# The up-projections of a latent attention as rounded high and low parts, with their weights earlier in the ring

## The chip, the cores and the metric

The kernel runs on one core of a Trainium2 chip, as one program. The time is that of one execution on the device, in microseconds (us); less is better. A core has TensorE (PE: matmuls, with the loads of their weights as PEld), VectorE (DVE), ScalarE (ACT), GpSimd (POOL) and SyncE (SP, which here issues the transfers from memory). Each engine runs its own instructions in order; between engines they wait for each other through counting semaphores.

## The reference

The program runs 512 tokens of width 1024, in float32, through two blocks. The first has two layers, each a projection of the normed input into 19 parts, four mixers beside each other (latent attention, differential attention, sparse attention with an index, a short convolution), gates, and an output projection. The second block (gated feed-forward, attention, attention to a memory, gated feed-forward) is not touched here. What is touched is the start of the latent attention:

```python
def _mla(cq, ckv, krope, qa_g, w_uq, kva_g, w_ukv, cos, sin):
    B, S, _ = cq.shape
    H = GROUP_HEADS                                     # 4
    q = (_rmsnorm(cq, qa_g) @ w_uq).reshape(B, S, H, MLA_NOPE + MLA_ROPE)       # 256 -> 4 x (64 + 32)
    ...
    kv = (_rmsnorm(ckv, kva_g) @ w_ukv).reshape(B, S, H, MLA_NOPE + MLA_V)      # 128 -> 4 x (64 + 64)
    k_nope, v = kv[..., :MLA_NOPE], kv[..., MLA_NOPE:]
```

The latents `cq` (256 wide) and `ckv` (128 wide) are parts of the first projection. The three products with `w_uq` and the two halves of `w_ukv` are the up-projections.

## The kernel before

**Matmuls.** Nearly all projections are made from rounded parts: a float32 operand is split into a high part, rounded to the format that TensorE multiplies in one go (`rounded(...)`, fp32r in the profile), and a low part, the rounded rest; three matmuls (high by high, high by low, low by high) add up to the product. The up-projections are the exception: they multiply plain float32 (`up_q`, `up_k`, `up_v`).

**The ring of weights.** Weights come in blocks of 128 x 1024 into a ring of four slots (`ring`). `TAKE` is the order of a layer's 44 blocks, so the slot of a block is its place in `TAKE` modulo four, and SyncE fetches block i + 4 when the job that used block i is done (`SLOT_JOB`). ScalarE makes the high part of a block (`whi`, two buffers, L1876), GpSimd its low part in two halves of 512 columns (L839), written over the block in its slot (`wlo` lies on `ring`). The blocks of the up-projections (`UK`, `UV`, `UQ`) are in `RAW`: no parts are made of them.

**Jobs.** A layer starts with fixed jobs (QI0, QI1 for the index, KR, CQ0, CQ1, CKV for the latents, BQ0, BK0, VT0). Then come 34 steps (`s`), each with the attention of some units (scores, transposes of the probabilities, products with the values) and fills: pieces of further projections from the list `FILLERS`, dealt out by a planner (`fill_plan`). Both kernels have the same plan. Step 0 is filled with BQ1; step 1 with UK0, UK1, UV0, UV1 and the start of BK1; step 2 ends BK1, copies a block of values (VN0) and starts VT1; then come UQ0 and UQ1, GT0 (gate block 0), UQ2.

**What sets the order around the change.** The scores of step s wait until the row minima of step s - 1 are taken (`min_ready`), which VectorE does. VectorE's first minimum in layer 0 waits until GpSimd has set the mask of the bias tables, which it does behind BK1's low part:

```python
dve.wait_ge(bias1_masked, 2)                       # ahead of step 0's minima
...
prepare_after("VT0")                               # on POOL: BK1's low part
if L == 0:
    mask_bias1()
after_low(SLOT_OF["BK1"])
```

The scores of step 2 use banks in which UK1 and UV0 lay, and wait for ScalarE's copies of these (`up_out`). VectorE scales the latents by their norms (L2601, `latent_ready`) before the up-projections.

Of the kernel before, what the change touches and what calls it, by code (L numbers as in the profile page):

```python
# [75 lines left out]
TAKE = ("QI0", "QI1", "KR", "KI", "CQ0", "CQ1", "CKV", "BQ0", "BK0", "VT0", "BQ1", "BK1", "UK", "UV", "VT1", "UQ",  # L76
# [14 lines left out]
SLOT_JOB = [JOB[{"UQ": "UQ2", "UK": "BK1", "UV": "BK1", "KI": "KR"}.get(name, name)] for name in TAKE]  # L91
# [220 lines left out]
LAYER_KA, LAYER_QA, LAYER_UP = 12, 7, 5  # L312
# [105 lines left out]
def build(nc, x, wstream, params, gains, tab1, tab2, hot1, hot2, rope, ident_in, mem, lines1, lines2, out):  # L418
    ctx = ExitStack()
    with ctx:  # L420
# [83 lines left out]
        cqn, ckvn = cqT, ckT[:, 0, :]  # L504
        at_v = at[0]
        vA, vBC = view(NT, 4 * HD), view(NT, 8 * HD)
        dBC = view(4, S)
# [312 lines left out]
        def _(pool):  # L820
# [69 lines left out]
            def layer(L):  # L890
# [36 lines left out]
                pool.wait_ge(kA_ready, L * LAYER_KA + 4)  # L927
# [27 lines left out]
                def low_a(which, h):  # L955

                    if which == "K" and h < 2:
                        pool.wait_ge(up_out, L * LAYER_UP + 5)
# [100 lines left out]
        def _(pe):  # L1059
# [113 lines left out]
            for L in range(DEPTH):  # L1173
# [39 lines left out]
                def turn_v(n):  # L1213

                    wait_out(pe, L, f"VT{n}")
                    if n == 0:
                        pe.wait_ge(up_out, L * LAYER_UP + 4)
# [76 lines left out]
                def up_q(n):  # L1294

                    w, b = raw_slot("UQ"), proj[bank_of(L, f"UQ{n}")]
                    pe.wait_ge(uq_loaded, 80 * (L + 1))
                    bank_free(f"UQ{n}")
                    for k in range(2):
                        block = 2 * ((n + 2) % 3) + k  # L1300
                        mm = pe.matmul(b[:, :], w[:, block * P:(block + 1) * P], cqn[:, k, :], start=(k == 0), stop=(k == 1))  # L1301
                    mm.then_inc(job_done, 1)

                def up_k(pair):

                    w, b = raw_slot("UK"), UP_BANK[f"UK{pair}"]
                    pe.wait_ge(latent_ready, L * 3 + 3)
                    pe.matmul(b[:, :], w[:, pair * P:(pair + 1) * P], ckvn, start=True, stop=True).then_inc(up_done, 1)

                def up_v(half):  # L1310

                    w, b = raw_slot("UV"), UP_BANK[f"UV{half}"]
# [44 lines left out]
                def scores(s):  # L1357
# [10 lines left out]
                    if s == B_STEPS:  # L1368
                        wait_out(pe, L, "UQ1", "UQ2")
                        pe.wait_ge(kA_ready, L * LAYER_KA + 8)  # L1370
                    if s == B_STEPS + 4:
                        pe.wait_ge(kA_ready, L * LAYER_KA + 12)
# [4 lines left out]
                    if quad_step(s):  # L1377
                        if s == 2:
                            pe.wait_ge(up_out, L * LAYER_UP + 3)
# [472 lines left out]
        def _(act):  # L1852
# [81 lines left out]
            for L in range(DEPTH):  # L1934
# [89 lines left out]

                prepare_after("VT0")
# [17 lines left out]
                def high_a(which, pair):  # L2043

                    heads = slice(2 * pair, 2 * pair + 2)
                    if which == "K":
                        act.wait_ge(up_out, L * LAYER_UP + (pair + 1))
                        act.wait_ge(kA_ready, L * LAYER_KA + 4)
# [62 lines left out]
                for s in range(LAST_STEP):  # L2111
# [268 lines left out]
        def _(dve):  # L2380
# [111 lines left out]
            for L in range(DEPTH):  # L2492
# [112 lines left out]
                stage_v(0)  # L2605

# [45 lines left out]
                def o_out(o):  # L2652
# [3 lines left out]
                    if branch == "B":  # L2656
                        if pair == 0:
                            dve.wait_ge(kA_ready, L * LAYER_KA + 4)
# [557 lines left out]
```

## Time and profile before

| | us |
|---|---|
| median of 3 runs | 1757.62 |
| lowest, highest | 1757.21, 1757.74 |
| profiled execution, its own time | 1759.74 |
| its span, from the first to the last instruction | 1757.9 |
| TensorE busy | 1749.2 |
| VectorE busy | 1032.4 |
| ScalarE busy | 757.8 |
| GpSimd busy | 421.5 |

Busy times are those of the profiled execution. Its mean granted TensorE clock is 0.998 of full speed. TensorE holds 99% of the chain of work that ended last. A matmul's row shows its whole passage, and successive ones overlap; the distance of two starts says what one costs in a steady flow.

### The profile page before, as it was taken

Reading aid. Unit: us, or ns where it says so; the run is one execution under the profiler, and the core shown is the slowest. Engines: PE = TensorE matmul, PEld = TensorE weight load, DVE = VectorE, ACT = ScalarE, POOL = GpSimd, SP = SyncE. Lnnn points to the kernel's source line nnn. Section 1 sums busy time; section 2 is a strip of 40 time slices with the busy share of each in tenths; the row PEclk is TensorE's granted clock in tenths of the full one; section 3 lists DMA queues with packets and bytes.
Section 4 is the critical chain, followed back from the end, with each engine's and each line's share of the span. In section 5 each row is a group of like instructions: output and inputs, shape, how many; then the busy total and the mean of one; then the engine's idle time right before and its main releaser. Section 6 shows DMA issues by size and latency. Waiting matters only on the chain.

```text
span 1757.9 us, 25383 instructions
## 1 busy us (share of the span) xinstructions
PE 1749.2 (100%) x9298; PEld 1435.9 (82%) x9298; DVE 1032.4 (59%) x2170; ACT 757.8 (43%) x1396; POOL 421.5 (24%) x326
## 2 busy tenths in 40 slices
PE   9999999999999999999999999999999999999998
PEld 7778878777887888888888888889888888888887
DVE  4888776688877665555433455445756655555333
ACT  6466644546564523233233455556434322222222
POOL 4545553454644500000000332330200200000000
PEclk9999999999999999999999999999999999999999
DMA  6432123323212343333333422223322333333332
GB/s 192 129 100 73 49 65 93 96 68 105 73 49 73 103 132 96 98 96 98 102 108 103 155 61 84 85 84 109 96 73 61 91 100 97 95 95 95 102 103 94
DMA packets 54421, 166.18 MB, mean 95 GB/s; under 512 B 10200, under 2 KB 10712, under 8 KB 54328
## 3 DMA queue, kind: packets, MB, share of 16 engines
q1 hardware_dynamic: 53032, 162.12, 30.6%
q10 hardware_dynamic: 1296, 2.84, 0.5%
q8 instruction: 56, 0.92, 0.2%
q14 instruction: 37, 0.30, 0.1%
HBM read 162.25 MB, written 2.17 MB: 94 GB/s over the span
## 4 chain that ended last, share of the span: by engine, by line
PE 99%; DMA 0%; DVE 0%; ACT 0%; ACTq 0%; POOL 0%; issue 0%; DVEq 0%
PE proj L1113 80%; PE turned L1427 2%; PE o L1449 2%; PE proj L1591 1%; PE proj L1584 1%; PE o L1692 1%; PE o L1792 1%; PE score L1397 1%; PE turned L1079 1%; PE turned L1671 1%; PE score L1781 1%; PE proj L1301 1%; PE turned L1654 1%; PE score L1386 1%; PE score L1654 0%; PE score L1269 0%
## 5 line engine op out<-in xcount | busy, mean ns | idle before, releaser
L1113 PE MATMUL proj<-hhi,whi 128*128 128x512 f32 x1456 | 582.6, 400 | 0.0
L1113 PE MATMUL proj<-hhi,wlo 128*128 128x512 f32 x1456 | 568.4, 390 | 0.0
L1113 PE MATMUL proj<-hlo,whi 128*128 128x512 f32 x1456 | 567.4, 390 | 0.0
L1876 ACT ACTIVATE whi<-ring 128x1024 fp32r<-128x1024 f32 x279 | 295.4, 1059 | 623.7 <-PE proj L1113 602.3
L2384 DVE TENSOR_TENSOR wlo<-ring,whi 128x1024 fp32r<-128x1024 f32 x199 | 243.2, 1222 | 161.2 <-ACT whi L1876 160.7
L1113 PEld LDWEIGHTS proj<-hhi,whi 128*128 128x128 f32 x1456 | 274.0, 188 | 63.6 <-issue 10.4
L1113 PEld LDWEIGHTS proj<-hhi,wlo 128*128 128x128 f32 x1456 | 273.4, 188 | 58.6
L1113 PEld LDWEIGHTS proj<-hlo,whi 128*128 128x128 f32 x1456 | 274.1, 188 | 53.5 <-issue 0.7
L839 POOL TENSOR_TENSOR wlo<-ring,whi 128x512 fp32r<-128x512 f32 x160 | 215.5, 1369 | 339.9 <-ACT whi L1876 339.9
L857 POOL TENSOR_TENSOR prob<-prob 128x512 f32<-128x512 f32 x36 | 56.9, 1581 | 872.2 <-ACT prob L1872 872.2
L1902 ACT ACTIVATE prob<-prob,negmax 128x256 f32<-128x256 f32 (+3 forms) x208 | 114.0, 550 | 74.1 <-DVE negmax L2457 73.4
L1113 PE MATMUL proj<-inner_hi,whi 128*128 128x512 f32 x352 | 136.9, 389 | 0.0
L1113 PE MATMUL proj<-inner_lo,whi 128*128 128x512 f32 x352 | 136.9, 389 | 0.0
L1113 PE MATMUL proj<-inner_hi,wlo 128*128 128x512 f32 x352 | 136.9, 389 | 0.0
L2457 DVE CUSTOM_DVE_ANT_0 prob<-score,arena 128x256 f32<-128x256 f32 (+3 forms) x148 | 60.6, 446 | 72.9 <-PE score L1654 61.0
L2468 DVE TENSOR_TENSOR tmp<-proj,R 128x512 f32<-128x512 f32 x48 | 33.2, 691 | 117.4 <-PE proj L1113 115.1
L1113 PE MATMUL proj<-yhi,whi 128*128 128x512 f32 x245 | 96.7, 395 | 0.1
L1113 PE MATMUL proj<-yhi,wlo 128*128 128x512 f32 x245 | 95.7, 390 | 0.0
L1113 PE MATMUL proj<-ylo,whi 128*128 128x512 f32 x245 | 95.2, 389 | 0.0
L2813 DVE TENSOR_TENSOR tmp<-tmp,proj 128x512 f32<-128x512 f32 x44 | 30.3, 688 | 103.7 <-PE proj L1113 103.5
L1113 PEld LDWEIGHTS proj<-inner_hi,wlo 128*128 128x128 f32 x352 | 66.1, 188 | 13.8
L1113 PEld LDWEIGHTS proj<-inner_hi,whi 128*128 128x128 f32 x352 | 66.1, 188 | 13.8
(379 smaller groups left out, 2436.9 us busy)
## 6 DMA issues: line engine op xcount, KB each, us to landing
ring<-wstream SPq DMA_DIRECT2D x285, 512.0 KB, 3.6
arena<-lines SPq DMA_DIRECT2D x28, 256.0 KB, 5.7
arena<-x ACTq DMA_DIRECT2D x4, 512.0 KB, 6.3
out<-arena SPq DMA_DIRECT2D x8, 256.0 KB, 2.9
arena<-mem SPq DMA_DIRECT2D x1, 1024.0 KB, 8.5
ring<-wstream SPq DMA_DIRECT2D x12, 64.0 KB, 2.2
ring<-wstream ACTq DMA_DIRECT2D x2, 256.0 KB, 7.7
arena<-rope SPq DMA_DIRECT2D x4, 128.0 KB, 6.4
```

The source lines that it names most:

```text
L839: return pool.tensor_tensor(rounded(wlo[:, s, cols]), ring[:, s, cols], whi[:, h, cols], ALU.subtract)
L857: pool.tensor_tensor(sq[:, 3, :], sq[:, 0, :] if c == 1 else sq[:, 3, :], sq_last if c == KC - 1 else sq[:, c % 3, :], ALU.add).then_inc(s ...
L1079: mm = pe.matmul(to[:, col + n * t:col + n * (t + 1)], chunk[:, t * P:(t + 1) * P], w, start=(first and t == 0), stop=False, skip_group_ch ...
L1113: mm = pe.matmul(b, rounded(w), rounded(rhs(v, k)), start=(first and n == 0 and p == 0), stop=(last and n == len(blocks) - 1 and p == 2))
L1427: mm = pe.transpose(turn_bank(g)[:, kb * P:(kb + 1) * P], prob[:, (2 * s + n) % 4, kb * P:(kb + 1) * P], ident[:, :])
L1449: mm = pe.matmul(opsum[o % 2][h * HD:(h + 1) * HD, qb * P:(qb + 1) * P], v, pT[:, (g - 1 + h) % 4, kb * P:(kb + 1) * P], start=(kb == 0), ...
L1876: act.activation(rounded(dst), src, ACT.Copy, scale=scale).then_inc(ready, 1)
L1902: act.activation(prob[:, i, 0:W], prob[:, i, 0:W], ACT.Exp, bias=negmax[:, i:i + 1], scale=-1.0, accum_out=rowsum[:, i:i + 1] if total is ...
L2384: dve.tensor_tensor(rounded(wlo[:, s, :]), ring[:, s, :], whi[:, h, :], ALU.subtract).then_inc(lo_ready, 1)
L2457: dve.tensor_tensor_reduce(prob[:, i, 0:W], src[:, 0:W], bias, 1.0, 3e38, ALU.add, ALU.min, negmax[:, i:i + 1]).then_inc(min_ready, 1)
L2468: return dve.tensor_tensor(dst, src, factors, ALU.mult)
L2813: dve.tensor_tensor(tmp[:, s, :], tmp[:, s, :], proj[(j + 1) % 2][:, :], ALU.mult)\
```

## The change

The three up-projections are made from rounded parts like the others: each plain matmul becomes three rounded ones (`up_q`: 2 to 6 in a job; `up_k`: 1 to 3; `up_v`: 2 to 6). For this ScalarE rounds the latents and the three weights, VectorE makes the low parts of the key latent and of the keys' and values' weights, GpSimd those of the query latents and the queries' weights. The high parts lie where factors of the norm lay, the low parts of the weights in their ring slots. In `TAKE`, UK and UV move ahead of BK1, so BK1's block goes from slot 3 to slot 1 and is fetched when VT0 is done, no longer when BQ0 is; the slots of UK and UV are free for UQ and GT0 once UK and UV are done. The semaphores' counts grow accordingly.

```diff
-TAKE = ("QI0", "QI1", "KR", "KI", "CQ0", "CQ1", "CKV", "BQ0", "BK0", "VT0", "BQ1", "BK1", "UK", "UV", "VT1", "UQ",
+TAKE = ("QI0", "QI1", "KR", "KI", "CQ0", "CQ1", "CKV", "BQ0", "BK0", "VT0", "BQ1", "UK", "UV", "BK1", "VT1", "UQ",
...
-SLOT_JOB = [JOB[{"UQ": "UQ2", "UK": "BK1", "UV": "BK1", "KI": "KR"}.get(name, name)] for name in TAKE]
+SLOT_JOB = [JOB[{"UQ": "UQ2", "UK": "BQ1", "UV": "BQ1", "KI": "KR"}.get(name, name)] for name in TAKE]
...
@@ gpsimd @@
                 after_low(SLOT_OF["BK1"])
                 pool.wait_ge(relu_ready, L * IDX_UNITS + IDX_UNITS)
+                pool.wait_ge(up_out, L * LAYER_UP + 4)
+                for k in range(2):
+                    pool.tensor_tensor(rounded(cqn_lo[:, k, :]), cqn[:, k, :], cqn_hi[:, k, :], ALU.subtract).then_inc(kA_ready, 1)
+                pool.wait_ge(kA_ready, L * LAYER_KA + 2)
                 for h in range(4):
                     pool.tensor_tensor(kA[rows, h, :], krope[rows, 0, :], krope[rows, 1, :], ALU.add).then_inc(kA_ready, 1)
...
+                def low_queries():
+
+                    slot = SLOT_OF["UQ"] % RING
+                    pool.wait_ge(up_out, L * LAYER_UP + 9)
+                    for cols in (slice(4 * P, 6 * P), slice(0, 4 * P)):
+                        pool.tensor_tensor(rounded(wlo[:, slot, cols]), ring[:, slot, cols], uq_hi[:, cols], ALU.subtract).then_inc(kA_ready, 1)
...
                         prepare_after(name)
+                        if name == "UV1":
+                            low_queries()
...
@@ tensor, up_q @@
-                    pe.wait_ge(uq_loaded, 80 * (L + 1))
+                    pe.wait_ge(kA_ready, L * LAYER_KA + (7 if n == 0 else 8))
...
-                        mm = pe.matmul(b[:, :], w[:, block * P:(block + 1) * P], cqn[:, k, :], start=(k == 0), stop=(k == 1))
+                        for p, (w, v) in enumerate(((uq_hi[:, cols], cqn_hi), (uq_hi[:, cols], cqn_lo), (wlo[:, slot, cols], cqn_hi))):
+                            mm = pe.matmul(b[:, :], rounded(w), rounded(v[:, k, :]), start=(k == 0 and p == 0), stop=(k == 1 and p == 2))
...
@@ tensor, up_k @@
-                    pe.wait_ge(latent_ready, L * 3 + 3)
-                    pe.matmul(b[:, :], w[:, pair * P:(pair + 1) * P], ckvn, start=True, stop=True).then_inc(up_done, 1)
+                    pe.wait_ge(latent_ready, L * LAYER_LATENT + 5)
+                    for p, (w, v) in enumerate(((uk_hi[:, cols], ckvn_hi), (uk_hi[:, cols], ckvn_lo), (wlo[:, slot, cols], ckvn_hi))):
+                        mm = pe.matmul(b[:, :], rounded(w), rounded(v), start=(p == 0), stop=(p == 2))
...
@@ tensor, up_v @@
+                    pe.wait_ge(latent_ready, L * LAYER_LATENT + 6)
                     for t in range(2):
-                        tok = (2 * half + t) * P
-                        mm = pe.matmul(b[:, t * 256:(t + 1) * 256], ckvn[:, tok:tok + P], w[:, 0:2 * P], start=True, stop=True)
+                        tok = slice((2 * half + t) * P, (2 * half + t + 1) * P)
+                        for p, (v, w) in enumerate(((ckvn_hi, uv_hi), (ckvn_hi, wlo[:, slot, 0:2 * P]), (ckvn_lo, uv_hi))):
+                            mm = pe.matmul(b[:, t * 256:(t + 1) * 256], rounded(v[:, tok]), rounded(w), start=(p == 0), stop=(p == 2))
...
@@ scalar @@
+                def high_queries():
+
+                    w = raw_loaded("UQ")
+                    act.wait_ge(uq_loaded, 80 * (L + 1))
+                    high(w[:, 0:6 * P], uq_hi, up_out)
+
+                act.wait_ge(latent_ready, L * LAYER_LATENT + 3)
+                high(ckvn, ckvn_hi, up_out)
+                high(raw_loaded("UK")[:, 0:2 * P], uk_hi, up_out)
+                high(raw_loaded("UV")[:, 0:2 * P], uv_hi, up_out)
+                high(cqn, cqn_hi, up_out)
                 prepare_after("VT0")
...
+                    if s == 1:
+                        high_queries()
...
@@ vector @@
                 stage_v(0)
+                dve.wait_ge(up_out, L * LAYER_UP + 1)
+                dve.tensor_tensor(rounded(ckvn_lo), ckvn, ckvn_hi, ALU.subtract).then_inc(latent_ready, 1)
+                for n, (name, w_hi) in enumerate((("UK", uk_hi), ("UV", uv_hi))):
+                    slot = SLOT_OF[name] % RING
+                    dve.wait_ge(up_out, L * LAYER_UP + (n + 2))
+                    dve.tensor_tensor(rounded(wlo[:, slot, 0:2 * P]), ring[:, slot, 0:2 * P], w_hi, ALU.subtract).then_inc(latent_ready, 1)
```

ScalarE's instructions between the jobs BK0 and BQ1 of layer 0, where the four new roundings come in. `wload0` to `wload3` say that the block in that ring slot has landed; the row with `whi` is BK1's rounding, the two rows after it are the exponentials of step 0. Before:

```order
L1876 ACTIVATE bk_hi_60<-arena 128x512 [waits job_free1]
L2017 ACTIVATE arena<-arena 128x2 [waits lam_step]
L1876 ACTIVATE whi<-ring 128x1024 [waits job_done,wload3]
L1902 ACTIVATE prob,arena<-prob,negmax 128x128 [waits min_ready]
L1902 ACTIVATE prob,rowsum<-prob,negmax 128x128 [waits min_ready]
```

and now:

```order
L1900 ACTIVATE bk_hi_60<-arena 128x512 [waits job_free1]
L2041 ACTIVATE arena<-arena 128x2 [waits lam_step]
L1900 ACTIVATE latent_hi_67<-arena 128x512 [waits latent_ready]
L1900 ACTIVATE factors2_53<-ring 128x256 [waits wload3]
L1900 ACTIVATE factors2_53<-ring 128x256 [waits wload0]
L1900 ACTIVATE latent_hi_67<-arena 128x1024
L1900 ACTIVATE whi<-ring 128x1024 [waits job_done,wload1]
L1926 ACTIVATE prob,arena<-prob,negmax 128x128 [waits min_ready]
L1926 ACTIVATE prob,rowsum<-prob,negmax 128x128 [waits min_ready]
```

BK1's rounding now stands behind four others and waits for another slot.

GpSimd's instructions of layer 0 from BK1's low part (the first two rows) to VT1's. The memsets set the mask, the rows of 32x512 are the rope sums. Before:

```order
L839 TENSOR_TENSOR wlo_49<-ring,whi 128x512 [waits hi_ready]
L839 TENSOR_TENSOR wlo_49<-ring,whi 128x512
L885 MEMSET arena 128x512
L888 MEMSET arena 64x13x64 [waits bias1_masked,bias1_loaded]
L926 TENSOR_TENSOR arena<-arena 32x512 [waits relu_ready,pool_lo_ready]
L926 TENSOR_TENSOR arena<-arena 32x512 x3
L945 TENSOR_TENSOR bq_lo_61<-arena,bq_hi_59 128x512 [waits bhi_ready,kA_ready]
L839 TENSOR_TENSOR wlo_49<-ring,whi 128x512 [waits hi_ready,b_ready]
L839 TENSOR_TENSOR wlo_49<-ring,whi 128x512
```

and now, up to the first low part of the queries' weights:

```order
L843 TENSOR_TENSOR wlo_49<-ring,whi 128x512 [waits hi_ready]
L843 TENSOR_TENSOR wlo_49<-ring,whi 128x512
L889 MEMSET arena 128x512
L892 MEMSET arena 64x13x64 [waits bias1_masked,bias1_loaded]
L931 TENSOR_TENSOR cq_lo_63<-arena,latent_hi_67 128x512 [waits up_out,relu_ready,pool_lo_ready]
L931 TENSOR_TENSOR cq_lo_63<-arena,latent_hi_67 128x512
L934 TENSOR_TENSOR arena<-arena 32x512 [waits kA_ready]
L934 TENSOR_TENSOR arena<-arena 32x512 x3
L960 TENSOR_TENSOR bq_lo_61<-arena,bq_hi_59 128x512 [waits bhi_ready,kA_ready]
L843 TENSOR_TENSOR wlo_49<-ring,whi 128x512 [waits hi_ready,b_ready]
L843 TENSOR_TENSOR wlo_49<-ring,whi 128x512
L942 TENSOR_TENSOR wlo_49<-ring,factors_52 128x256 [waits up_out]
```

Two subtractions come in between the mask and the rope sums, and two more behind VT1's low part.

## Rows read from the trace of the kernel before

**Rows 1.** The page's busy times: engine, us (share of the span), instructions.

```profile
PE 1749.2 (100%) x9298; PEld 1435.9 (82%) x9298; DVE 1032.4 (59%) x2170; ACT 757.8 (43%) x1396; POOL 421.5 (24%) x326
```

**Rows 2.** TensorE's waits after 60 us: line, releaser, total us, times, longest.

```profile
PE turned L1079 <- ACT pT L2206: 0.2, 1, 0.2
```

**Rows 3.** Chain of work, 50 to 130 us: start us, us, what.

```profile
75.42 5.67 PE proj L1113 x24
...
81.57 1.91 PE turned L1308 x4
83.48 1.73 PE o L1315 x8
85.21 3.41 PE proj L1113 x15
...
101.40 1.72 PE proj L1301 x4
```

**Rows 4.** Timeline of TensorE near 1070 us: start us, us, instruction.

```profile
1070.04 0.28 PE L1584 MATMUL proj<-memhi,wlo 128*128 128x256 f32 x1
1070.16 0.28 PE L1584 MATMUL proj<-memhi,whi 128*128 128x256 f32 x1
```

**Rows 5.** Timeline of TensorE, layer 0 and, last row, layer 1.

```profile
81.02 0.33 PE L1397 MATMUL score<-bk_hi,bq_hi 32*128 32x128 f32 x2
...
88.55 0.50 PE L1386 MATMUL score<-bk_hi,bq_hi 32*128 32x512 f32 x2
...
92.05 0.48 PE L1113 MATMUL proj<-hhi,whi 128*128 128x512 f32 x1
...
391.78 0.48 PE L1113 MATMUL proj<-hhi,whi 128*128 128x512 f32 x1
```

**Rows 6.** SyncE's issue, its time to landing, and all such loads.

```profile
74.97 0.33 SPq L751 DMA_DIRECT2D ring<-wstream  x1
...
ring<-wstream SPq DMA_DIRECT2D x1, 512.0 KB, 3.5
...
DMA to landing us min/median/max: 3.4/3.6/7.4
```

**Rows 7.** Timeline of ScalarE, layer 0; brackets: idle before, and its end.

```profile
75.03 1.06 ACT L1876 ACTIVATE whi<-ring 128x1024 fp32r<-128x1024 f32 x1 [4.16 <-PE proj L1113]
...
84.38 0.63 ACT L1876 ACTIVATE bq_hi<-arena 128x512 fp32r<-128x512 f32 x1 [3.03 <-DVE arena L2469]
...
87.34 0.60 ACT L2065 ACTIVATE arena<-o 128x512 f32<-128x512 f32 x1
```

**Rows 8.** Timeline of GpSimd, layer 0.

```profile
76.17 2.55 POOL L839 TENSOR_TENSOR wlo<-ring,whi 128x512 fp32r<-128x512 f32 x2 [3.75 <-ACT whi L1876]
...
79.31 0.79 POOL L888 MEMSET arena<- 64x832 f32 x1
80.17 4.97 POOL L926 TENSOR_TENSOR arena<-arena 32x512 f32<-32x512 f32 x4
85.22 1.29 POOL L945 TENSOR_TENSOR bq_lo<-arena,bq_hi 128x512 fp32r<-128x512 f32 x1
```

**Rows 9.** Timeline of VectorE, layer 0 and, last row, layer 1.

```profile
73.57 2.05 DVE L2601 SCALAR_TENSOR_TENSOR arena<-arena,par,turned 128x512 f32<-128x512 f32 x3
...
80.13 0.29 DVE L2457 CUSTOM_DVE_ANT_0 prob<-score,arena 128x128 f32<-128x128 f32 x1 [2.52 <-issue]
...
377.25 0.28 DVE L2457 CUSTOM_DVE_ANT_0 prob<-score,arena 128x128 f32<-128x128 f32 x1
```

**Rows 10.** TensorE's timeline; stretches: length, busy PE, PEld, DVE, ACT, POOL, granted clock.

```profile
194.79 1.84 PE L1079 MATMUL proj<-halves,tmp 128*128 128x2 f32 x16
...
190.00:200.00 10.00, 10.00 (x70) 8.73 (x69) 7.28 (x25) 4.22 (x10) 3.81 (x4) 0.90 0.20 56
200.00:210.00 10.00, 10.00 (x62) 8.28 (x61) 5.45 (x23) 7.62 (x24) 4.20 (x3) 0.93 0.10 19
490.00:500.00 10.00, 10.00 (x75) 8.67 (x74) 7.31 (x28) 4.42 (x10) 3.80 (x4) 1.00 0.19 54
```

More of the change, by code:

```diff
@@ L311 @@
          B_STEPS: (("K", 2), ("K", 3)), B_STEPS + 1: (("Q", 2),), B_STEPS + 2: (("Q", 3),)}
-LAYER_KA, LAYER_QA, LAYER_UP = 12, 7, 5
+LAYER_KA, LAYER_QA, LAYER_UP, LAYER_LATENT = 16, 7, 10, 6
 LAST_STEP = FILL_STEPS + 4
@@ L504, in build @@
         cqn, ckvn = cqT, ckT[:, 0, :]
+        cqn_lo, ckvn_lo = cq_lo, ck_lo[:, 0, :]
+        uk_hi, uv_hi, uq_hi = factors[1][:, 0, 0:2 * P], factors[1][:, 0, 2 * P:4 * P], factors[0][:, :, :].rearrange("p a b -> p (a b)")[:, 0:6 * P]
         at_v = at[0]
         vA, vBC = view(NT, 4 * HD), view(NT, 8 * HD)
+        latent_hi = over("latent_hi", "arena", [P, 3, S], at[0])
+        cqn_hi, ckvn_hi = latent_hi[:, 0:2, :], latent_hi[:, 2, :]
         dBC = view(4, S)
@@ L957, in low_a @@
                     if which == "K" and h < 2:
-                        pool.wait_ge(up_out, L * LAYER_UP + 5)
+                        pool.wait_ge(up_out, L * LAYER_UP + 10)
                     else:
@@ L1216, in turn_v @@
                     if n == 0:
-                        pe.wait_ge(up_out, L * LAYER_UP + 4)
+                        pe.wait_ge(up_out, L * LAYER_UP + 8)
                     if n == 1:
@@ L1300, in up_q @@
                         block = 2 * ((n + 2) % 3) + k
-                        mm = pe.matmul(b[:, :], w[:, block * P:(block + 1) * P], cqn[:, k, :], start=(k == 0), stop=(k == 1))
+                        cols = slice(block * P, (block + 1) * P)
+                        for p, (w, v) in enumerate(((uq_hi[:, cols], cqn_hi), (uq_hi[:, cols], cqn_lo), (wlo[:, slot, cols], cqn_hi))):
+                            mm = pe.matmul(b[:, :], rounded(w), rounded(v[:, k, :]), start=(k == 0 and p == 0), stop=(k == 1 and p == 2))
                     mm.then_inc(job_done, 1)
                 def up_k(pair):
-                    w, b = raw_slot("UK"), UP_BANK[f"UK{pair}"]
-                    pe.wait_ge(latent_ready, L * 3 + 3)
-                    pe.matmul(b[:, :], w[:, pair * P:(pair + 1) * P], ckvn, start=True, stop=True).then_inc(up_done, 1)
+                    slot, b = SLOT_OF["UK"] % RING, UP_BANK[f"UK{pair}"]
+                    cols = slice(pair * P, (pair + 1) * P)
+                    pe.wait_ge(latent_ready, L * LAYER_LATENT + 5)
+                    for p, (w, v) in enumerate(((uk_hi[:, cols], ckvn_hi), (uk_hi[:, cols], ckvn_lo), (wlo[:, slot, cols], ckvn_hi))):
+                        mm = pe.matmul(b[:, :], rounded(w), rounded(v), start=(p == 0), stop=(p == 2))
+                    mm.then_inc(up_done, 1)
                 def up_v(half):
-                    w, b = raw_slot("UV"), UP_BANK[f"UV{half}"]
+                    slot, b = SLOT_OF["UV"] % RING, UP_BANK[f"UV{half}"]
+                    pe.wait_ge(latent_ready, L * LAYER_LATENT + 6)
                     for t in range(2):
-                        tok = (2 * half + t) * P
-                        mm = pe.matmul(b[:, t * 256:(t + 1) * 256], ckvn[:, tok:tok + P], w[:, 0:2 * P], start=True, stop=True)
+                        tok = slice((2 * half + t) * P, (2 * half + t + 1) * P)
+                        for p, (v, w) in enumerate(((ckvn_hi, uv_hi), (ckvn_hi, wlo[:, slot, 0:2 * P]), (ckvn_lo, uv_hi))):
+                            mm = pe.matmul(b[:, t * 256:(t + 1) * 256], rounded(v[:, tok]), rounded(w), start=(p == 0), stop=(p == 2))
                     mm.then_inc(up_done, 1)
@@ L1369, in scores @@
                         wait_out(pe, L, "UQ1", "UQ2")
-                        pe.wait_ge(kA_ready, L * LAYER_KA + 8)
+                        pe.wait_ge(kA_ready, L * LAYER_KA + 12)
                     if s == B_STEPS + 4:
-                        pe.wait_ge(kA_ready, L * LAYER_KA + 12)
+                        pe.wait_ge(kA_ready, L * LAYER_KA + 16)
                     if s == C_STEP:
@@ L1378, in scores @@
                         if s == 2:
-                            pe.wait_ge(up_out, L * LAYER_UP + 3)
+                            pe.wait_ge(up_out, L * LAYER_UP + 7)
                         if quad_out(s) == 0 and quad_out(s - 2) == 1:
@@ L2023, in copy_v, with raw_loaded @@
                         .then_inc(v_copied, 1)
+                def raw_loaded(name):
+                    i = SLOT_OF[name]
+                    act.wait_ge(wload[i % RING], L * (16 * LAYER_SLOTS // RING) + 16 * (i // RING + 1))
+                    return ring[:, i % RING, :]
+                def high_queries():
[7 more added lines that the diff above has]
+                high(cqn, cqn_hi, up_out)
                 prepare_after("VT0")
@@ L2046, in high_a @@
                     if which == "K":
-                        act.wait_ge(up_out, L * LAYER_UP + (pair + 1))
-                        act.wait_ge(kA_ready, L * LAYER_KA + 4)
+                        act.wait_ge(up_out, L * LAYER_UP + (pair + 5))
+                        act.wait_ge(kA_ready, L * LAYER_KA + 6)
                         src, dst = kA[0:96, heads, :], kA_hi[pair][0:96, :, :]
```

6 lines of the change are left out of this document (3 added, 3 removed).

## The prediction

> **What bounds the kernel now.** Read the page first: TensorE is busy for 1749.2 of 1757.9 us [rows 1]. The list of waits then says whether it ever stands still: after the first 60 us it waited once, for 0.2 us [rows 2]. So the time is the sum of TensorE's instructions, in their order. What the change takes from them is gained, a wait that it adds there is paid in full, and work on the other engines counts only where TensorE comes to wait for it. The third view is the chain of work where the up-projections run in layer 0 [rows 3]; the fourth, the timelines of all engines from 70 to 103 us [rows 5 to 9], which tell how late each input may be. Layer 1 repeats them 299.7 us later (VT1 begins at 92.05 and at 391.78 [rows 5]), without the two memsets of the bias mask, which only layer 0 has.
>
> **TensorE's own work.** Today the two keys' jobs take 1.91 us and the two values' jobs 1.73 us [rows 3]. Of the 3.64, 0.21 is the passage out of the scores before them: behind the same kind of scores 24 rounded matmuls took 5.67 us, while 15 in steady flow took 3.41, or 0.227 each, and 5.67 - 24 x 0.227 = 0.21. That passage stays; 3.43 us goes. In its place come six rounded matmuls of 512 columns, 6 x 0.227 = 1.36, and twelve of 256 columns, whose starts lie 0.12 us apart elsewhere [rows 4], 1.44. Gain 0.63 us. A job of the queries takes 1.72 us [rows 3] and becomes six matmuls of 512: 1.36, a gain of 0.36, three times in a layer: 1.08. Both layers: 2 x (0.63 + 1.08) = **3.4 us less TensorE work**. Were nothing late, the change would gain that, 0.19%.
>
> **What comes late: BK1's weights.** In the ring's old order BK1's block was fetched when BQ0 was done, three jobs before its rounding; now it is fetched when VT0 is done. That issue, UV's today, stands at 74.97 us, and landed 3.5 us later [rows 6], at 78.5. ScalarE's rounding of BK1, which today begins at 75.03 [rows 7], so begins at 78.5: 3.5 us late. ScalarE's four new roundings stand ahead of it, but they are done by then: the scaled latents are ready at 73.57 + 2.05 = 75.6 [rows 9]; a rounding of 512 columns takes 0.63 us and one of 1024 columns 1.06 [rows 7], so with 0.63 as the bound for each of the two narrow ones all four end by 75.6 + 3 x 0.63 + 1.06 = 78.6 at most. They cost nothing as long as the load is the later one.
>
> GpSimd works in order, and behind BK1's rounding stands its low part (76.17 us today) and then, in layer 0, the memsets of the bias mask, which end at 80.10 [rows 8]. VectorE's first row minimum waits for just that by the program (the profile names no releaser): it starts at 80.13 after 2.52 us of idling [rows 9]. All this moves by 3.5 us, to 83.6, and the two minima of step 0, 0.28 us each, end at about 84.1. TensorE's scores of step 1 wait for these minima by the program; today they start at 81.02 [rows 5] with the minima done by 80.7. They will start at about 84.2: **layer 0 loses 3.2 us**, with TensorE idle. Layer 1 has no mask; there the three new subtractions of VectorE move its first minimum from 377.25 [rows 9] by some 1.5 us to 378.8, and its scores of step 1, at 81.02 + 299.7 = 380.7, still have over a microsecond to spare.
>
> **The second wait of layer 0.** The scores of step 2 need the copies of both keys' jobs and of one values' job out of PSUM; the last ends at 87.34 + 0.60 = 87.94 [rows 7] and the scores start at 88.55 [rows 5]. These copies stand behind a rounding that waits for VectorE [rows 7], and VectorE's line is now 3.5 us late, so they end at 91.44. TensorE comes there at 88.55 + 3.2 - 0.63 = 91.1: a wait of 0.4 us, which takes most of the 0.63 back.
>
> **The wait of layer 1: VT1's low part.** On GpSimd two subtractions of the queries' latents come in, ahead of the four rope sums and of VT1's low part. In the clock times of layer 0, mask left out: BK1's rounding ends at 78.5 + 1.06 = 79.6, its low part takes 2.55 us (to 82.2), the new pair 2 x 1.29 (as BQ1's low part [rows 8], the same shape; to 84.8), the rope sums 4.97 (to 89.8), BQ1's low part 1.29 (to 91.1), the first half of VT1's low part half of 2.55 (to 92.4). TensorE wants VT1 at 92.05 - 0.63 = 91.4 [rows 5]. **Layer 1 waits about 1.0 us**, 1.1 with the gaps between instructions. In layer 0 the mask adds 1.4 us to GpSimd's line, but TensorE is 3.0 us late there, so nothing is to be waited for.
>
> **Costed at nothing.** VectorE's three subtractions (some 1.5 us) lie where it idled, or ahead of minima that are not yet needed; if that cover went, layer 1 would pay what they take beyond it at step 1. GpSimd's low parts of the queries' weights (2 us by their width) follow on VT1's second half and are done some 3.3 us after its first; the queries' first job comes after all of VT1, 24 x 0.227 = 5.4 us after it. ScalarE's rounding of those weights (0.8 us by the width) stands ahead of a copy of probabilities that TensorE multiplies two steps later. The queries' six loads now go out once the keys' jobs are done and no longer behind BK1's job, and gate block 0 behind them earlier too: a gain without a taker, since TensorE did not wait for either [rows 2].
>
> **The clock.** The trace shows what low activity costs: in two rows of 10 us around 200 us the granted clock averages 0.90 and 0.93 [rows 10], that is, it stood at the lower of its two levels (1.2 for 2.4 GHz) for a part of each; 10 x 0.10 + 10 x 0.07 = 1.7 us were lost. Before it fell TensorE had not idled at all: it had run sixteen matmuls of two columns in 1.8 us, and short ones [rows 10]. A stop of 3.2 us is idler still, so I expect a fall in layer 0 at or behind it. Its price lies between nothing (if it falls early enough to pass within the stop) and 1.7 us; I take 1.3, near the row. A slower TensorE also swallows the 0.4 us wait of step 2, so the net is 0.9. The Trainium skill (TensorE: Matmul & The Clock Gate, "Why this matters for your kernels") warns that idle gaps between bursts of matmuls send the clock back to its lower level; it is the rule that speaks most against this change. By that rule alone the fall would be certain, and at the full 1.7 us the sum below would be 1.4 - 0.4 + 1.7 = 2.7 us, or 1760.3. The rows leave it open, as one of two like stretches fell and the other did not. Without any fall the sum is 0.9 us lower.
>
> **Sum.** Layer 0: +3.2 - 0.63 + 0.4 - 1.08 + 0.1 (the later stages of VectorE, whose slack of under 2 us towards TensorE is now thin) = +2.0. Layer 1: -0.63 + 1.1 - 1.08 = -0.6. Together +1.4 us, with the clock +2.2. The profiled execution took 1759.74 us for its span of 1757.9 and would take 1761.9; it lies 2.1 us above the median of the runs, 1757.62, and it is the difference that carries over: **1759.8 us**. What a measurement of this kernel can tell from no change is 0.2%, 3.5 us, so 1754.1 to 1761.1 counts as the same.
>
> **Rivals.**
> Stops as forecast, but no fall of the clock: 1757.6 + 1.4 = 1759.0. For it: the same stretch in layer 1 left the clock at 1.00 [rows 10].
> Slower: BK1's block lands later than 3.5 us. Loads of this kind landed in 3.4 to 7.4 us, with 3.6 as the median [rows 6]. Each microsecond is paid in full twice, at step 1 of layer 0 and at VT1 in layer 1. From 4.2 us on the result is slower: +2.2 + 2 x 0.7 = +3.6, 1761.2; at 5 us, 1762.8. For it: the load now gates at once, with no slack. Against it: at this very place the load of today landed in 3.5 us, with nothing else under way. A slower run of GpSimd's six subtractions would act in the same direction, in layer 1 alone.
> Faster: neither stop shows, because the rounding of BK1 or the mask is not in TensorE's way; then the 3.4 us stay: 1757.6 - 3.4 = 1754.2, at the edge of what can be told. It decides where the load lands in under 0.5 us, or where TensorE's scores had over 3 us of slack; both speak against the rows, which give 0.4.
>
> **How the numbers follow.** Forecast with the fall of the clock 0.46; without it 0.24; late landing or slower subtractions 0.23; no stops 0.07. The first two lie between 1758.0 and 1761.1. To leave out no more than 2 in 10 the range runs from 1757.4 (a shorter stop, no fall) to 1762.8 (a landing of 5 us). Slower: the 0.23 and the upper tail of the first, 0.27; faster 0.06; the same 0.67.
>
> **What would show it.** In the changed kernel's profile: ScalarE's rounding of BK1 some 3.5 us later and released by a DMA; VectorE's first minimum of layer 0 near 83.6; a wait of TensorE of about 3.2 us before the scores of step 1 in layer 0, and of about 1 us before VT1 in layer 1, released by GpSimd; keys' and values' jobs of 2.8 us, queries' jobs of 1.36; the granted clock below 1 between 82 and 90 us. I am wrong if TensorE shows no wait there, if the rounded jobs are not shorter, or if a wait appears further on, at the queries' jobs or at gate block 0, which have least slack after that.

## The result, and the profile after

| | before | changed |
|---|---|---|
| median of 12 runs each, us | 1757.58 | **1761.66** |
| lowest, highest | 1756.98, 1759.39 | 1760.17, 1763.87 |
| profiled execution, its own time | 1759.74 | 1763.87 |
| its span | 1757.9 | 1762.0 |

The ratio is 1.0022, with a 95% interval of 1.0014 to 1.0030: the change costs 4.1 us, by the interval 2.5 to 5.3; forecast were 2.2 us. Among the runs further down, two single executions of 3516.53 and 2477.15 us lie far outside the rest and are left out of the medians.

The page's busy times of the changed kernel, which answer to [rows 1], and the list of TensorE's waits after 60 us, which answers to [rows 2]:

```profile
PE 1747.2 (99%) x9322; PEld 1440.4 (82%) x9322; DVE 1036.4 (59%) x2176; ACT 762.8 (43%) x1406; POOL 430.9 (24%) x334
```

```profile
PE score L1421 <- DVE negmax L2500: 2.9, 1, 2.9
PE proj L1130 <- POOL wlo L843: 1.0, 1, 1.0
PE o L1473 <- ACT arena L2046: 0.9, 1, 0.9
```

TensorE is busy 2.0 us less and the span is 4.1 us longer: what was gained in work was lost in waiting, most of it TensorE's, and 1.6 us of it behind TensorE's last matmul (below). Beside the one wait of 0.2 us there are now three of 1 to 3 us. TensorE's timeline, which answers to [rows 5], shows them in their places: step 1's and step 2's scores in layer 0, VT1 in layer 1, and, in layer 0 again, the products with the values:

```profile
83.29 0.33 PE L1421 MATMUL score<-bk_hi,bq_hi 32*128 32x128 f32 x2 [2.89 <-DVE negmax L2500]
...
91.74 0.50 PE L1410 MATMUL score<-bk_hi,bq_hi 32*128 32x512 f32 x2
...
395.39 0.47 PE L1130 MATMUL proj<-hhi,whi 128*128 128x512 f32 x1 [1.00 <-POOL wlo L843]
...
145.00 0.44 PE L1473 MATMUL o<-pT,arena 128*64 128x128 f32 x4 [0.92 <-ACT arena L2046]
```

Its rows are read against [rows 5] less 0.7 us: this execution is that much ahead from its first 20 us on (VectorE scales the latents at 72.88, below, and at 73.57 in [rows 9]). The scores of step 1 start 2.3 us later than before (81.02), so 3.0 were lost; those of step 2 3.2 later (88.55); VT1 of layer 1 3.6 later (391.78). The timelines of ScalarE, GpSimd and VectorE in layer 0 tell why, and answer to [rows 7 to 9]:

```profile
77.67 1.06 ACT L1900 ACTIVATE whi<-ring 128x1024 fp32r<-128x1024 f32 x1 [0.51 <-DMA ring<-wstream]
...
78.81 2.51 POOL L843 TENSOR_TENSOR wlo<-ring,whi 128x512 fp32r<-128x512 f32 x2 [7.08 <-ACT whi L1900]
...
81.91 0.78 POOL L892 MEMSET arena<- 64x832 f32 x1
82.66 2.52 POOL L931 TENSOR_TENSOR cq_lo<-arena,latent_hi 128x512 fp32r<-128x512 f32 x2
...
72.88 2.05 DVE L2644 SCALAR_TENSOR_TENSOR arena<-arena,par,turned 128x512 f32<-128x512 f32 x3
...
76.84 0.68 DVE L2650 TENSOR_TENSOR ck_lo<-arena,latent_hi 128x512 fp32r<-128x512 f32 x1
77.44 0.75 DVE L2654 TENSOR_TENSOR wlo<-ring,factors 128x256 fp32r<-128x256 f32 x2
82.73 0.29 DVE L2500 CUSTOM_DVE_ANT_0 prob<-score,arena 128x128 f32<-128x128 f32 x1 [4.54 <-issue]
```

BK1's rounding starts at 77.67, released by the DMA of its weights; GpSimd's low part follows, then the mask, which ends at 82.69, and at 82.73 VectorE's first minimum. In the chain of work each of the three jobs of the queries now takes 1.40 us, which answers to the 1.72 of [rows 3]; the first is

```profile
101.10 1.40 PE proj L1320 x6
```

The granted clock by stretches (columns as in [rows 10]):

```profile
80.00:85.00 5.00, 2.11 (x13) 1.46 (x12) 2.23 (x14) 0.88 (x4) 4.88 (x6) 1.00 0.34 105
85.00:90.00 5.00, 5.00 (x22) 4.51 (x21) 4.75 (x20) 2.96 (x6) 4.92 (x5) 0.66 0.35 71
200.00:210.00 10.00, 10.00 (x61) 8.41 (x60) 7.03 (x26) 5.57 (x18) 6.62 (x4) 0.83 0.07 29
```

The first stretch holds the stop, the second the up-projections at a mean of 0.66, that is, part of it at 1.2 GHz for 2.4; 5 x 0.34 = 1.7 us were lost in it. The third is the fall that [rows 10] show for before as well.

### The profile page after: what moved, and what is told of

Same layout as the page of the kernel before. It is cut to its first block, busy times and chain, and to the rows that moved or that the text cites. A ratio compares the mean times of both kernels' runs of the same rounds, so it can differ in the third digit from the quotient of the medians.

```text
span 1762.0 us, 25453 instructions
## 1 busy us (share of the span) xinstructions
PE 1747.2 (99%) x9322; PEld 1440.4 (82%) x9322; DVE 1036.4 (59%) x2176; ACT 762.8 (43%) x1406; POOL 430.9 (24%) x334
## 4 chain that ended last, share of the span: by engine, by line
PE 95%; POOL 1%; DVE 1%; issue 1%; ACT 0%; DMA 0%; ACTq 0%; POOLq 0%; DVEq 0%
PE proj L1130 77%; PE turned L1451 2%; PE o L1473 2%; PE proj L1615 1%; PE proj L1608 1%; PE o L1716 1%; PE o L1816 1%; PE turned L1695 1%; PE score L1805 1%; PE score L1421 1%; PE turned L1096 1%; PE turned L1678 1%; POOL wlo L843 1%; PE proj L1320 0%; PE score L1678 0%
```

## Experiments

Each run stands beside runs of the kernel before on the same chip. Both kernels spread: the runs of before over 2.4 to 2.8 us, those of the changed one over 3.7 and 3.8. The intervals of the ratios are therefore wide, about 0.1% to each side, and a wait of 1 us is judged by the profile.

| | median, us | to before | ratio, 95% interval |
|---|---|---|---|
| the change again | 1762.29 | +4.5 | 1.0024 (1.0014 to 1.0033) |
| order alone | 1762.87 | +4.8 | 1.0026 (1.0016 to 1.0036) |
| mask first | 1759.47 | +1.4 | 1.0005 (0.9996 to 1.0014) |
| pair later | 1762.19 | +4.4 | 1.0023 (1.0013 to 1.0032) |
| mask first, pair later | 1755.53 | -2.4 | 0.9988 (0.9979 to 0.9997) |
| the same again | 1756.17 | -1.6 | 0.9988 (0.9979 to 0.9997) |
| stop filled | 1760.59 | +2.6 | 1.0016 (1.0007 to 1.0025) |
| keys' low part later | 1763.44 | +5.5 | 1.0027 (1.0017 to 1.0038) |
| all three moved | 1755.76 | -2.2 | 0.9988 (0.9979 to 0.9996) |
| BK1 between UK and UV | 1759.99 | +2.0 | 1.0008 (0.9999 to 1.0017) |
| the same, kept apart | 1755.12 | -2.6 | 0.9986 (0.9977 to 0.9995) |

**Order alone.** The kernel before with the new order:

```diff
-... "BQ1", "BK1", "UK", "UV", "VT1", "UQ",
+... "BQ1", "UK", "UV", "BK1", "VT1", "UQ",
```

> The kernel before with the new order of TAKE alone: BK1's block is fetched when VT0 is done, the up-projections stay plain float32. My theory: the order alone makes the stop, about 3.2 us before the scores of step 1 in layer 0, with a fall of the granted clock behind it; no wait at VT1 in layer 1, since the two new subtractions of GpSimd are not there; 1757.6 + 3.2 + about 1.3 = 1762. Rival (the stop comes from the four new roundings and the new subtractions ahead of BK1's parts): no stop, 1757.6.

Its list of waits and its stretches:

```profile
PE score L1397 <- DVE negmax L2457: 3.1, 1, 3.1
```

```profile
80.00:85.00 5.00, 2.00 (x8) 1.37 (x9) 2.52 (x15) 0.88 (x4) 4.80 (x6) 0.80 0.35 105
85.00:90.00 5.00, 5.00 (x11) 2.98 (x10) 4.74 (x22) 3.25 (x6) 3.68 (x3) 0.52 0.00 0
```

The stop is that of the order. The clock's fall costs more here, up to 5 x 0.20 + 5 x 0.48 = 3.4 us; why it stays low for longer is not shown. No wait stands before VT1.

**Mask first.** The changed kernel, GpSimd's mask moved:

```diff
+                if L == 0:
+                    mask_bias1()
                 prepare_after("VT0")
-                if L == 0:
-                    mask_bias1()
```

> The changed kernel with one edit: GpSimd sets the bias mask of layer 0 before BK1's low part instead of behind it. My theory (the stop before the scores of step 1 is BK1's late landing, passed on through GpSimd's line to the mask and to VectorE's first minimum): that stop of 2.9 us disappears, with it the fall of the granted clock between 80 and 90 us, but VT1's low part is now late in layer 0 as well (about 0.9 us, as in layer 1); in all 3 us or more less than the changed kernel, 1756.2 to 1758.4. Rival (VectorE's first minimum is late because of its own three new subtractions, or because of the late scores): the stop stays at 2 to 3 us and the time at 1761 to 1762.

The waits of this kernel:

```profile
PE proj L1130 <- POOL wlo L843: 2.1, 2, 1.1
```

The stop of step 1 is gone; instead VT1 now waits in both layers, 1.0 and 1.1 us (the 0.9 us at the values stays). The profile is as the first theory had it; the median lies 1.1 us above its range, the lowest run, 1757.58, within.

**Pair later.** The pair of subtractions moves from ahead of the rope sums into `low_queries` (behind VT1's low part), and the counts of `kA_ready` with it:

```diff
-                for k in range(2):
-                    pool.tensor_tensor(rounded(cqn_lo[:, k, :]), ...)
...
                 def low_queries():
+                    for k in range(2):
+                        pool.tensor_tensor(rounded(cqn_lo[:, k, :]), ...)
```

> The changed kernel with one edit: GpSimd's two subtractions of the queries' latents moved from ahead of the rope sums to behind VT1's low part. My theory: only the wait before VT1 of layer 1 goes; the stop before step 1 of layer 0 and its fall of the clock stay; 1.0 us less than the changed kernel, about 3 us above the kernel before. Rival (BK1's late low part alone makes VT1's low part late): the wait stays, and so does the time.

The waits, and GpSimd's line in layer 1:

```profile
PE score L1420 <- DVE negmax L2499: 3.0, 1, 3.0
PE o L1472 <- ACT arena L2045: 0.9, 1, 0.9
PE score L1409 <- ACT arena L2105: 0.4, 1, 0.4
```

```profile
389.15 2.59 POOL L843 TENSOR_TENSOR wlo<-ring,whi 128x512 fp32r<-128x512 f32 x2
391.71 1.29 POOL L937 TENSOR_TENSOR cq_lo<-arena,latent_hi 128x512 fp32r<-128x512 f32 x1
```

The wait before VT1 is gone, and none came at the queries' jobs. The fall of the clock that I expected behind the stop is not in this profile; with it gone, the 0.4 us before the scores of step 2 shows. The median doesn't show that the wait before VT1 went: the runs lie between 1758.62 and 1763.59, those of the change again between 1760.12 and 1763.92. The lowest run is 1.5 us lower; by time alone this run is inconclusive.

**Both edits.** What each edit by itself leaves over, the other takes:

> The changed kernel with the bias mask ahead of BK1's low part, and the two subtractions of the queries' latents moved on GpSimd from ahead of the rope sums to behind VT1's low part. My theory (what makes VT1's low part late in both layers is this pair ahead of it): the two waits before VT1 of 1.0 to 1.1 us each that the kernel with the mask alone moved still had are gone, no new one appears at the first job of the queries; 2.1 us less than that kernel, so 0.7 us below the kernel before. Rival (BK1's late low part alone makes VT1's low part late, or the queries' low parts now come late): 1 us or more of wait stays, and the time is at or above the kernel before.

> The changed kernel with the mask and the pair moved, once more, to set it beside the changed kernel on one chip. My theory: no wait of TensorE but the one of 0.9 us before the values' matmuls, 2 to 3 us below the kernel before, and 5 to 7 us below the changed kernel. Rival (its lead was that of the chip or the hour): within 1 us of the kernel before.

In both runs one wait is left after 60 us beside the 0.2 us of [rows 2], the one at the values:

```profile
PE o L1472 <- ACT arena L2045: 0.9, 1, 0.9
```

This kernel beats both: 1.6 to 2.4 us below the one before, some 6 below the changed one (1756.17 to 1762.29 on one chip).

**The change again.**

> The changed kernel once more, unaltered, to see which of its stops come in every execution. My theory (the stops follow from the order of the instructions): the waits before the scores of step 1 (2.9 us), before VT1 of layer 1 (1.0) and before the values' matmuls near 145 us (0.9) and the fall of the granted clock between 80 and 90 us are there again; the time is 3.3 to 4.1 us above the kernel before. Rival (the wait of 0.9 is a chance of one execution): it is not there, and the time is about 1 us lower.

All waits are there again, and with them one of 0.4 us before the scores of step 2, but not the fall of the clock:

```profile
PE score L1421 <- DVE negmax L2500: 3.1, 1, 3.1
PE proj L1130 <- POOL wlo L843: 1.0, 1, 1.0
PE o L1473 <- ACT arena L2046: 0.9, 1, 0.9
PE score L1410 <- ACT arena L2106: 0.4, 1, 0.4
```

```profile
85.00:90.00 5.00, 5.00 (x29) 4.37 (x28) 4.75 (x21) 2.55 (x5) 4.92 (x5) 1.00 0.31 66
```

So the stops belong to the program, the fall to the execution. In the five profiles of kernels that stop for 2.9 to 3.1 us at step 1 the clock fell at the stop or behind it in three and stood in two (this one and pair later). None of the eight profiles of kernels without this stop, the kernel before among them, has a fall between 80 and 90 us.

**Stop filled.** 

```diff
                     else:
+                        if s == 1 and L == 0:
+                            pe.wait_ge(latent_ready, 5)
+                            for _ in range(13):
+                                pe.matmul(UP_BANK["UK0"][:, :], rounded(uk_hi[:, 0:P]), rounded(ckvn_hi), start=True, stop=True)
                         pe.wait_ge(min_ready, L * LAYER_SM + 2 * s)
```

> The changed kernel with 13 rounded matmuls of 512 columns (2.95 us) of TensorE ahead of the scores of step 1 in layer 0, whose result is overwritten: they fill the stop, so that TensorE doesn't idle there. My theory (the granted clock falls because of the stop): the scores start when they did, the granted clock stays at 1.00 between 80 and 90 us, the up-projections take 2.8 us instead of 4.2, and the wait of 0.4 us before the scores of step 2 that the slower TensorE swallowed shows again: 1.0 us less than the changed kernel, or 3.1 us above the kernel before. Rival (the clock falls for the short matmuls around it, stop or no stop): the clock falls all the same and the time stays 4.1 us above the kernel before.

```profile
PE score L1414 <- ACT arena L2110: 0.4, 1, 0.4
```

```profile
80.00:85.00 5.00, 5.00 (x26) 3.80 (x25) 2.36 (x14) 0.88 (x4) 4.88 (x5) 1.00 0.34 105
85.00:90.00 5.00, 5.00 (x29) 4.16 (x27) 4.75 (x21) 3.09 (x6) 4.92 (x5) 1.00 0.40 79
```

As the first theory had it: no fall, the 0.4 us shows, 2.6 us above the kernel before where the changed kernel is 4.1 and 4.5 above it, and the runs lie closer, 1760.01 to 1762.06. As the fall is not in every execution, one profile without it is weak evidence, and the intervals of the ratios overlap. The granted clocks of all runs say more. Each run's mean granted clock is on record, to 0.001: its average is 0.9977 and 0.9976 in the two sets of the changed kernel, 0.9988 in the kernel before (32 and 31 runs), and 0.9989 with the stop filled. So the changed kernel loses 0.0010 to 0.0011 of 1760 us, 1.8 to 2.0 us, more to the clock than the kernel before, and with TensorE busy through the stop it does not. (These averages hold the stretch behind the last matmul too, where a low clock costs nothing; so the 1.8 to 2.0 us are an estimate.)

**Keys' low part later.** The unforeseen wait of 0.9 us at the values:

```diff
-A_LOW = {ROPE_STEPS[-1] + 3: (("K", 0),), ROPE_STEPS[-1] + 4: (("K", 1),), ...
+A_LOW = {ROPE_STEPS[-1] + 4: (("K", 0), ("K", 1)), ...
```

> The changed kernel with the low part of the first head's keys, 96x512, one step later on GpSimd. My theory (the unforeseen wait of 0.9 us before the values' matmuls at 145 us is VectorE's scaling of the probabilities, 1.77 us for 0.86, beside this subtraction of GpSimd, which began 0.05 us before it): VectorE's scaling takes about 0.9 us again and the wait is gone, 0.9 us less than the changed kernel, or 3.2 us above the kernel before. Rival (VectorE is late there for another reason, such as the 0.3 us by which it lags): the scaling is as long as now, or the wait stays, and the time stays 4.1 us above the kernel before.

First the place in the kernel before, VectorE's and GpSimd's timelines:

```profile
136.91 0.86 DVE L2643 SCALAR_TENSOR_TENSOR prob<-prob,rrow 128x512 f32<-128x512 f32 x1
...
137.18 1.75 POOL L962 TENSOR_TENSOR kA_lo<-arena,kA_hi 96x512 fp32r<-96x512 f32 x1
```

then in the changed kernel:

```profile
139.21 1.77 DVE L2692 SCALAR_TENSOR_TENSOR prob<-prob,rrow 128x512 f32<-128x512 f32 x1
...
139.16 1.27 POOL L977 TENSOR_TENSOR kA_lo<-arena,kA_hi 96x512 fp32r<-96x512 f32 x1
```

and in this one:

```profile
139.83 0.75 DVE L2692 SCALAR_TENSOR_TENSOR prob<-prob,rrow 128x512 f32<-128x512 f32 x1
...
148.69 2.99 POOL L977 TENSOR_TENSOR kA_lo<-arena,kA_hi 96x512 fp32r<-96x512 f32 x2
```

Before, VectorE's scaling began first: it took 0.86 us, and GpSimd's subtraction 1.75 for 1.27. In the changed kernel GpSimd began 0.05 us ahead of it; now VectorE's took 1.77. Behind it stand VectorE's next minima, ScalarE's exponentials and, behind these, its copy of the values (`copy_v`), for which TensorE waits. With GpSimd's instruction away the scaling takes 0.75 us and the wait is gone. The time did not fall with it: +5.5 us to the kernel before, where I expected +3.2 (its profile has the falls of the clock at 80 to 90 and at 200 to 210 us, 0.83 each, and the clocks of its runs average 0.9967). With the other two edits, too, it is neither better nor worse:

> The changed kernel with all three edits: the mask ahead of BK1's low part, the pair of subtractions behind VT1's low part, the first head's low part of the keys one step later. My theory: none of the four waits is left and the shorter work of TensorE shows, of which 3.4 us was forecast; by the other three runs' sums 1.6 us below the kernel before, 3.4 at best. Rival (each wait removed uncovers the next, since VectorE or GpSimd is now short of slack): it is not below the kernel before.

Only the wait of 0.2 us of [rows 2] is left there after 60 us. The lowest run, 1754.48, is 0.6 below that of mask first, pair later; the median is 0.2 above. Its profile has a fall of the clock at 490 to 500 us (0.83), which one of the two profiles without this edit has as well. Whether the wait removed raises the chance of that fall stays open.

**BK1 between UK and UV.** BK1's block is fetched early and rounded first, ahead of the new roundings:

```diff
-... "BQ1", "UK", "UV", "BK1", "VT1", "UQ",
+... "BQ1", "UK", "BK1", "UV", "VT1", "UQ",
...
+                prepare_after("VT0")
                 high(ckvn, ckvn_hi, up_out)
                 high(raw_loaded("UK")[:, 0:2 * P], uk_hi, up_out)
-                high(raw_loaded("UV")[:, 0:2 * P], uv_hi, up_out)
                 high(cqn, cqn_hi, up_out)
-                prepare_after("VT0")
+                high(raw_loaded("UV")[:, 0:2 * P], uv_hi, up_out)
```

> The changed kernel with BK1 between UK and UV in TAKE, so that its block is fetched when BK0 is done, and with ScalarE rounding BK1 ahead of the latents and UV last. My theory: no stop before step 1, no late low part before VT1 in either layer, all of the shorter work of TensorE kept: 1757.6 - 3.4 = 1754.2, 1753.8 to 1755.2. Rival (the queue of GpSimd is too long by the two new subtractions, or VectorE's new ones are in the way, wherever BK1's load stands): waits of about 1 us stay in each layer, 1756 or more.

I was wrong, by nearly 6 us. Its waits, then layer 1 on VectorE and GpSimd, and below these layer 0 on the same two:

```profile
PE score L1421 <- DVE negmax L2500: 1.6, 2, 0.9
PE o L1473 <- ACT arena L2046: 0.9, 1, 0.9
PE score L1410 <- ACT arena L2106: 0.8, 2, 0.4
```

```profile
375.65 1.11 DVE L2650 TENSOR_TENSOR ck_lo<-arena,latent_hi 128x512 fp32r<-128x512 f32 x1
376.69 2.94 DVE L2654 TENSOR_TENSOR wlo<-ring,factors 128x256 fp32r<-128x256 f32 x2
379.56 0.28 DVE L2500 CUSTOM_DVE_ANT_0 prob<-score,arena 128x128 f32<-128x128 f32 x1
...
374.91 3.01 POOL L843 TENSOR_TENSOR wlo<-ring,whi 128x512 fp32r<-128x512 f32 x2 [4.37 <-ACT whi L1900]
378.00 2.76 POOL L931 TENSOR_TENSOR cq_lo<-arena,latent_hi 128x512 fp32r<-128x512 f32 x2
```

```profile
80.50 0.29 DVE L2500 CUSTOM_DVE_ANT_0 prob<-score,arena 128x128 f32<-128x128 f32 x1 [0.80 <-issue]
...
76.08 3.00 POOL L843 TENSOR_TENSOR wlo<-ring,whi 128x512 fp32r<-128x512 f32 x2 [4.37 <-ACT whi L1900]
...
79.67 0.79 POOL L892 MEMSET arena<- 64x832 f32 x1
```

The load is early, VT1 does not wait, but the scores of step 1 do, in both layers (0.7 and 0.9 us), and those of step 2 after them. With the 0.9 us at the values that is 3.3 of the 5.8 us; where the rest lies is not settled. In layer 1 VectorE's three new subtractions took 4.05 us, against 1.43 where GpSimd was idle beside them (76.84 and 77.44 in the changed kernel, above): they waited for GpSimd's instructions, one after another, and the first minimum follows directly on them. In layer 0 it was not they that made the minimum late: VectorE idled for 0.80 us ahead of it, until the mask was set (79.67 + 0.79 = 80.46). The mask was late because BK1's rounding, now placed behind ScalarE's wait for the scaled latents, began at 74.94, 0.6 us later than before less the head start, and because GpSimd's low part took 3.00 us beside VectorE's subtractions, for 2.55 [rows 8]. The last kernel keeps the two engines apart (mask first, pair later, and a wait of GpSimd ahead of BK1's low part):

```diff
+                pool.wait_ge(latent_ready, L * LAYER_LATENT + 6)
                 prepare_after("VT0")
```

> The kernel with BK1 between UK and UV, with the mask ahead of BK1's low part, the pair of subtractions behind VT1's low part, and GpSimd starting BK1's low part only when VectorE has made its three new ones. My theory (in the kernel with BK1 between UK and UV, VectorE's new subtractions ran 1.5 to 2.6 us longer, 2.95 and 4.05 us for 1.43, because GpSimd's ran beside them, and that made the scores of step 1 late in both layers): VectorE's three take 1.43 us again, no wait is left before the scores of steps 1 and 2, and the time is like that of the changed kernel with the mask and the pair moved, 2.4 us below the kernel before. Rival (VectorE's subtractions are long for another reason, or their place ahead of the first minimum alone makes the scores late): waits of 0.7 us or more stay before the scores of step 1 in both layers, and the time is 1 to 2 us above the kernel before.

```profile
76.67 0.67 DVE L2650 TENSOR_TENSOR ck_lo<-arena,latent_hi 128x512 fp32r<-128x512 f32 x1
77.27 0.41 DVE L2654 TENSOR_TENSOR wlo<-ring,factors 128x256 fp32r<-128x256 f32 x1
78.01 0.42 DVE L2654 TENSOR_TENSOR wlo<-ring,factors 128x256 fp32r<-128x256 f32 x1 [0.34 <-ACT factors L1900]
78.36 0.28 DVE L2500 CUSTOM_DVE_ANT_0 prob<-score,arena 128x128 f32<-128x128 f32 x1
...
78.52 2.54 POOL L843 TENSOR_TENSOR wlo<-ring,whi 128x512 fp32r<-128x512 f32 x2 [5.58 <-DVE wlo L2654]
```

0.67 + 0.41 + 0.42 = 1.50 us; no wait before steps 1 and 2 is left (the 0.9 us at the values is). With 1755.12 us it has the lowest median of all, though not clear of that of mask first, pair later. GpSimd starts BK1's low part some 2.4 us later here (78.52 for 76.08), and VectorE's three are done before. In layer 1, which has no mask to move, it is the same: they take 1.52 us and end at 375.74, and GpSimd begins at 375.82. That is as the theory had it; what the wait of GpSimd does without the other two moves was not tried.

## Why the prediction was right or wrong

- **TensorE's work, -3.4 us.** Right. The matmuls of the keys' and values' jobs start 0.23 and 0.12 us apart at the full clock (the change again), and the queries' jobs take 1.40 for the forecast 1.36. The busy time fell by only 2.0 us because it holds one fall of the clock more (1.7).
- **Layer 0, step 1, +3.2.** Right in its chain and place: 2.9 and 3.1 us in two profiles, of the order alone (order alone), by way of the mask (mask first). ScalarE's rounding, GpSimd's low part, mask and minimum came as told, each 0.8 to 0.9 us ahead of the forecast time, of which 0.7 is this execution's head start.
- **Step 2, +0.4, swallowed by a fall.** Right both ways: 0.4 without the fall, none with it. (By the prediction's own figures it would be 0.3, 91.44 less 91.1.)
- **Layer 1, VT1, +1.0 to 1.1.** Right: 1.0, by the pair of subtractions (pair later).
- **The clock, +1.3.** Right in kind and place, too small in size. One fall cost the forecast's upper bound, 1.7, and over all executions the clock cost an estimated 1.8 to 2.0 us more than before (stop filled): part of the executions hold more than one fall (the profiled one, with a mean clock of 0.997, has two). The Trainium skill's rule (TensorE: Matmul & The Clock Gate, "Why this matters for your kernels"), that idle gaps send the clock back to its lower level, agrees with three of five profiles: it names what can happen here, not what must.
- **What failed: "the later stages of VectorE", +0.1, and "VectorE's three subtractions ... lie where it idled", at nothing.** I weighed slack in each engine's own line and left out that two engines hold each other up. The term was +0.9: at the values VectorE and GpSimd met 0.3 us apart from where they had met before. The same oversight was harmless for the three subtractions only because BK1's late load kept GpSimd idle beside them; with the early load they cost 0.9 us at step 1 of layer 1, and helped to make the mask late in layer 0 (BK1 between UK and UV).

With 0.9 in place of that 0.1 the sum is 1.4 - 0.1 + 0.9 = +2.2 without a fall (the stop filled, which has none at this place: +2.6). With the clock at 1.8 to 2.0, less up to 0.4 for the wait of step 2 that a fall swallows, it is +3.6 to +4.2; measured are 4.1 and 4.5. So the forecast was some 2 us too low, about half of it by each of the two terms; the time lies in the upper part of its range, which was left open for a late landing, and that did not occur: that the range held is in part luck. The time also lies above 1761.1, up to which the prediction counted a result as the same, and so in the case to which it gave 0.27. (Its own terms, 1.4 and 0.9, add up to 2.3 and not 2.2.)

On TensorE's line the two profiles give +3.2 (its last matmul ends at 1752.2 before and at 1754.7 now, 2.5 later, and 0.7 is the head start); the lowest runs of the two kernels also lie 3.2 apart. Of the 4.1 us between the profiled executions, 1.6 lies behind that matmul (5.7 us before, 7.3 now), where little but the last stores is left. In the change again the same stretch took 5.7 us; over the thirteen profiles it took 4.2 in one, 5.7 to 5.8 in eight and 7.1 to 7.4 in four. It varies from execution to execution, for a reason that is not shown, and a single time should be read with that in mind. The clock's share is seen in the runs: the five executions of the changed kernel at a mean clock of 0.999 took 1760.4 us in the mean, the ten at 0.997 or less 1763.1; none of the kernel before was below 0.998.

The rivals: a later landing did not occur (BK1's rounding began at 77.67, where 78.5 less the head start was forecast); that there would be no stops is refuted; stops with no fall at them are what part of the executions show.

## What to carry to other kernels

Before a load is moved down a ring's order, follow it through every engine that works on the block in order, and ask what unrelated work stands behind it there: here a mask that has nothing to do with the weights. Two small moves of such bystanders turned a loss of 4 us into a gain of 2. And an engine's idle time is not free room for a subtraction if GpSimd and VectorE then run at once: look for pairs that begin within each other.

## What was not expected of the hardware

An operation of VectorE with two inputs in SBUF (where the tiles lie that are not TensorE's results) and a subtraction of GpSimd did not run beside each other: whichever began second took longer by about the time that the other still needed (0.75 to 1.77 us, 1.27 to 1.75, 1.43 to 4.05 for three). VectorE's searches, of one input, ran at their usual 0.41, 0.54 and 0.68 us beside GpSimd's subtractions of the queries' latents (83.24 to 84.84 us in the changed kernel), and an operation with one of its two inputs in PSUM (where TensorE's results lie) took 0.67 us, no longer than elsewhere, beside GpSimd's rope sums (at 86.27 us there). This agrees with the Trainium skill (SBUF — State Buffer, "SBUF: two separate sides"), by which the two engines share a pair of ports that one of them holds for a whole instruction. And the clock's fall behind the same 3 us stop came in some executions and not in others.
